# Relative-bias mask laid out on the host, stacks made in separate high and low steps, and the index scores of branch A moved by one projection unit

## The chip, the cores and the metric

The kernel runs on one core of a Trainium2 chip. The metric is the device time of one execution in microseconds (us), taken as the median of several runs; less is better. One execution of the kernel before was also recorded by the hardware profiler, and all rows below come from it.

## What is computed

Two layers of one block, on 512 positions of width 1024 in float32. A layer takes an RMS norm, projects it (`w_in`) and feeds three branches:

```
logits = einsum('bqhd,bsd->bqhs', iqb, ik)             # branch A, index scores: 4 heads of 64
score  = einsum('bqhs,bqh->bqs', relu(logits), iwb)    # the 128 best keys of each query are kept
s      = einsum(q, k_sel) * scale; softmax; times v    # branch A: 8 heads, 2 key heads
s      = einsum(q, k) * scale + bias[None]             # branch B: 8 heads, bias by relative position,
                                                       # keys of later 64-position chunks excluded
branch C: an mLSTM in chunks, 4 heads of 128
x + merge(branches, gates) @ w_out
```

## The kernel before, in words

**Units.** The projections of a layer are cut into units of 128 output columns (U_IQ = 0, U_IK = 2, U_SMALL = 3, U_AK = 4, U_AV = 5, U_AQ = 6 to 9, U_BQ = 10, U_BK = 14, U_BV = 18, the C branch from 22, the z gates of branch A from 34). A unit is 24 matmuls of 128x512 on TensorE (L565): the weights and the activations are each kept as a rounded high part and a low part that is the rest, and each of eight chunks takes high by high, low by high and high by low. ScalarE (ACT) makes the high part of a unit's weights (L756) two units ahead and reads a unit's sum out of PSUM (L819), in this order; GpSimd (POOL) makes the low part (L515).

**One hand-written order.** `schedule()` (L72 to L210) writes one list of steps for a layer, SEQUENCE, and every engine goes through this same list and does its own part of each step. `interleave()` (L213) puts the steps that stand between two units into the 24 matmuls of the later one, in groups separated by CUT, at even distances. So a step's place in the list sets its place in the queue of each engine at once. An attention item n (0 to 31 branch A, 32 to 63 branch B, head h = (n - 32) // 4 and query tile t = n % 4) is pushed by `push(n)` (L78): ("scores", n), then exp of item n - 1, the turning of n - 2 and the values of n - 3. TensorE's score banks in PSUM are two, used in turn: the scores of item n wait until VectorE (DVE) has read item n - 2.

**Stacks.** A score matmul contracts over 128 rows: 64 rows of high part and 64 rows of low part, stacked in `iq_s`, `ik_s`, `ak_s`, `aq_s`, `bq_s`, `bk_s`. In one step, such as ("b_stack", h), ACT writes the high parts (L879, L881, counted by `stack_hi`), and DVE waits for them and writes the low parts (L1131 to L1138, counted by `stack_ready`); TensorE waits for the latter (L618, L629, L635). The step stands at item 29 + 4h, and head h of branch B begins at item 32 + 4h. The index stacks (L847 to L858, L1105 to L1114) stand after units 5 and 6, and the index scores of query tile 1 inside unit 7 (L111, L115 to L121). The index scores of tiles 2 and 3 are inside units 13 and 15 (INDEX_AT). The first stacks of branch A stand after unit 16 (L136), the others at items 2, 10 and 18 (STACK_AT, L68).

**Top keys.** 48 rounds ("topk", L1139 to L1149) of the 8 largest scores and their replacement run on DVE: ROUNDS (L65) says how many stand behind each unit from 7 to 16, and the rest are spread over the items 0 to 21.

**Ropes.** ("rope", u) turns a projection by position with four DVE instructions of 128x512 and a shuffle (L1085 to L1088). That of U_AK stands right ahead of the first index scores, those of units 6 to 9 two units behind their unit.

**Bias.** ("rel_bias", h): ACT issues the DMA of a head's 128x512 bias (L898), for head 0 and 1 after unit 16, for a later head h at item 27 + 4h, where DVE must have read the last item of head h - 2. DVE, in the same step, waits for the DMA and writes the excluded corner of 64x64 with a memset (L1169, L1170). The scores step of branch B adds the bias and takes the row maximum (L1185).

Of the kernel before, what the change touches and what calls it, by code (L numbers as in the profile page):

```python
# [64 lines left out]
ROUNDS = {7: 4, 8: 4, 9: 4, 10: 4, 11: 0, 12: 2, 13: 2, 14: 2, 15: 2, 16: 2}  # L65


STACK_AT = {2: ("aq_stack", 1), 10: ("aq_stack", 2), 18: ("aq_stack", 3), 26: ("b_stack", 0)}  # L68
STACK_AT.update({29 + 4 * h: ("b_stack", h) for h in range(1, HEADS)})


def schedule():  # L72
# [184 lines left out]
STACK, STACKS = order("iq_stack", "ik_stack", "ak_stack", "aq_stack", "b_stack")  # L257
DVE_STEPS = 267
# [21 lines left out]
def build(nc, x_in, w_full, w_mix, params_in, rel_in, gains_in, consts_in, out, x_kept):  # L280
    ctx = ExitStack()
    with ctx:
# [255 lines left out]
        def _(pe):  # L538
# [49 lines left out]
            for l in range(DEPTH):  # L588
                for kind, n in SEQUENCE:
# [25 lines left out]
                    elif kind == "index":  # L615
                        t, h = n
                        bank = scores_bank(l, step)
                        pe.wait_ge(stack_ready, l * STACKS + STACK[("ik_stack", 0)] + 1)  # L618
# [4 lines left out]
                    elif kind == "scores":  # L623
# [3 lines left out]
                        if branch == "a":  # L627

                            pe.wait_ge(stack_ready, l * STACKS + STACK[("aq_stack", t)] + 1)  # L629
# [4 lines left out]
                        elif branch == "b":  # L634
                            pe.wait_ge(stack_ready, l * STACKS + STACK[("b_stack", h)] + 1)  # L635
# [97 lines left out]
        def _(act):  # L733
# [24 lines left out]
            for l in range(DEPTH):  # L758
# [64 lines left out]
                for kind, n in SEQUENCE:  # L823
# [23 lines left out]
                    elif kind == "iq_stack":  # L847
# [8 lines left out]
                    elif kind == "ik_stack":  # L856
                        act.wait_ge(roped, l * ROPES + ROPE[("rope", U_IK)] + 1)
                        act.activation(ik_s[:, 0, :], ik[:, :], ACT.Copy).then_inc(stack_hi, 1)  # L858
                    elif kind == "ak_stack":
# [6 lines left out]
                    elif kind == "aq_stack":  # L866
# [7 lines left out]
                    elif kind == "b_stack":  # L874
# [4 lines left out]
                        act.activation(bq_s[n % 2][b:b + HD, :], bq[b:b + HD, n // 2, :], ACT.Copy)  # L879
# [108 lines left out]
        def _(dve):  # L988
# [46 lines left out]
            for l in range(DEPTH):  # L1035
# [9 lines left out]
                for kind, n in SEQUENCE:  # L1045
# [59 lines left out]
                    elif kind == "iq_stack":  # L1105
                        dve.wait_ge(stack_hi, l * STACKS + STACK[step] + 1)
# [5 lines left out]
                    elif kind == "ik_stack":  # L1112
                        dve.wait_ge(stack_hi, l * STACKS + STACK[step] + 1)
                        dve.tensor_tensor(ik_s[:, 1, :], ik[:, :], ik_s[:, 0, :].bitcast(F32), ALU.subtract).then_inc(stack_ready, 1)  # L1114
                    elif kind == "ak_stack":
                        dve.wait_ge(stack_hi, l * STACKS + STACK[step] + 1)
# [6 lines left out]
                    elif kind == "aq_stack":  # L1123
                        dve.wait_ge(stack_hi, l * STACKS + STACK[step] + 1)
# [5 lines left out]
                    elif kind == "b_stack":  # L1130
                        dve.wait_ge(stack_hi, l * STACKS + STACK[step] + 1)  # L1131
                        p, q = (0, HD) if n % 2 == 0 else (HD, 0)
                        dve.tensor_tensor(bq_s[n % 2][q:q + HD, :], bq[p:p + HD, n // 2, :], bq_s[n % 2][p:p + HD, :].bitcast(F32),
                                          ALU.subtract)
# [295 lines left out]
```

## Time and profile before

| | us |
|---|---|
| median of 3 runs (1436.21 to 1438.34) | 1437.28 |
| the profiled execution, its own time | 1437.05 |
| its span in the trace | 1435.2 |
| TensorE, matmuls busy | 1326.3 (92%) |
| DVE busy | 758.3 (53%) |
| ACT busy | 624.5 (44%) |
| POOL busy | 480.5 (33%) |
| mean granted clock of TensorE | 0.967 of full speed |

The span runs from the first to the last recorded instruction, so about 2 us of the profiled execution lie around it. The first layer fills the trace up to about 725 us and the second, of the same steps, the rest; the stretch that the change touches goes from about 54 to 386 us, and again from about 750 to 1081 us.

### The profile page before, as it was taken

What the parts mean: (1) busy time and instruction counts of PE and PEld (TensorE: products, weight loads), DVE (VectorE), ACT (ScalarE), POOL (GpSimd) and SP (SyncE); (2) the same over time, 40 slices, a digit from 0 to 9 for tenths busy, and PEclk for the clock granted to TensorE, in tenths of its full rate; (3) what the DMA queues carried; (4) which work ended last, traced back from release to release, by engine and by line L of the source; (5) the groups of instructions that cost most, each with busy time, mean ns of one, the idle gap of its engine ahead of it and who ended that gap; (6) DMA issues with size and microseconds to landing.
All of it is one profiled execution on the core that took longest, in us unless ns stands there. A gap on an engine that the chain in (4) does not pass through costs nothing.

```text
span 1435.2 us, 20030 instructions
## 1 busy us (share of the span) xinstructions
PE 1326.3 (92%) x6525; PEld 1106.4 (77%) x6525; DVE 758.3 (53%) x1460; ACT 624.5 (44%) x1119; POOL 480.5 (33%) x227
## 2 busy tenths in 40 slices
PE   5989898779999899999998989888899989999997
PEld 3768787668898688888876878777778868888886
DVE  5788787664445421211868877757453461212156
ACT  4434555656543332332343356564654343322332
POOL 2533221221113344444553432221111234444442
PEclk9999999999999999999999999999999999999999
DMA  6222211112132133323242222111111313323331
GB/s 234 75 73 91 74 57 45 52 59 67 43 105 69 57 95 92 99 94 110 76 174 76 74 95 68 45 52 54 51 62 51 110 51 102 95 88 102 93 105 58
DMA packets 37034, 117.42 MB, mean 82 GB/s; under 512 B 4064, under 2 KB 6496, under 8 KB 36448
## 3 DMA queue, kind: packets, MB, share of 16 engines
q1 hardware_dynamic: 34368, 111.37, 23.6%
q10 hardware_dynamic: 2592, 5.11, 1.1%
q8 instruction: 40, 0.66, 0.2%
q14 instruction: 34, 0.28, 0.1%
HBM read 110.18 MB, written 6.29 MB: 81 GB/s over the span
## 4 chain that ended last, share of the span: by engine, by line
PE 66%; DVE 19%; issue 6%; ACT 4%; DMA 2%; POOL 1%; DVEq 0%; ACTq 0%; SPq 0%; POOLq 0%
PE acc L565 54%; PE ps_o L674 3%; PE ps_t L661 2%; DVE score L1146 2%; DVE top L1144 1%; PE ps_t L652 1%; DVE prob L1185 1%; PE ps_o L681 1%; DMA rel<-rel 1%; PE ps_s L631 1%; DVE bk_lo_s L1136 1%; DVE aq_s L1127 1%; DVE att_c L1286 1%; ACT bk_hi_s L881 1%; DVE turn L1160 1%
## 5 line engine op out<-in xcount | busy, mean ns | idle before, releaser
L515 POOL TENSOR_TENSOR w_lo<-w_raw,w_hi 128x1024 fp32r<-128x1024 f32 (+1 forms) x212 | 468.3, 2210 | 922.4 <-ACT w_hi L756 922.4
L565 PE MATMUL acc<-h_hi,w_hi 128*128 128x512 f32 x1136 | 465.4, 410 | 0.1
L565 PE MATMUL acc<-h_lo,w_hi 128*128 128x512 f32 x1136 | 456.0, 401 | 0.0
L565 PE MATMUL acc<-h_hi,w_lo 128*128 128x512 f32 x1136 | 302.6, 401 | 1.2 <-POOL w_lo L515 1.2
L756 ACT ACTIVATE w_hi<-w_raw 128x1024 fp32r<-128x1024 f32 (+1 forms) x212 | 203.9, 962 | 129.7 <-PE acc L565 99.5
L565 PEld LDWEIGHTS acc<-h_hi,w_hi 128*128 128x128 f32 x1136 | 220.0, 194 | 42.3 <-ACT w_hi L756 1.1
L565 PEld LDWEIGHTS acc<-h_lo,w_hi 128*128 128x128 f32 x1136 | 220.1, 194 | 41.1
L565 PEld LDWEIGHTS acc<-h_hi,w_lo 128*128 128x128 f32 x1136 | 212.7, 192 | 43.9 <-POOL w_lo L515 2.0
L1299 DVE SCALAR_TENSOR_TENSOR gated<-prob,acc 128x512 f32<-128x512 f32 x16 | 11.0, 688 | 251.8 <-PE acc L565 251.8
L904 ACT ACTIVATE prob<-prob,neg_max 128x128 f32<-128x128 f32 (+3 forms) x128 | 70.9, 554 | 71.2 <-DVE neg_max L1185 70.7
L954 ACT ACTIVATE prob<-acc,par_half 128x512 f32<-128x512 f32 x48 | 33.0, 688 | 154.1 <-PE acc L565 154.1
L661 PE MATMUL ps_t<-consts,prob 128*128 128x128 f32 x320 | 59.2, 284 | 18.8 <-ACT prob L904 18.7
L928 ACT ACTIVATE prob_t<-ps_t 128x128 f32<-128x128 f32 (+3 forms) x128 | 54.2, 423 | 45.1 <-PE ps_t L661 44.6
L674 PE MATMUL ps_o<-bv,prob_t 128*128 128x64 f32 x320 | 45.8, 276 | 21.6 <-issue 21.3
L1144 DVE MAX8 top<-score 128x8 f32<-128x256 f32 (+2 forms) x96 | 53.8, 561 | 17.5 <-DVE neg_max L1185 8.6
L674 PEld LDWEIGHTS ps_o<-bv,prob_t 128*128 128x128 f32 x320 | 43.3, 201 | 24.5 <-issue 23.0
L661 PEld LDWEIGHTS ps_t<-consts,prob 128*128 128x128 f32 x320 | 39.8, 145 | 28.5 <-issue 24.0
L674 PE MATMUL ps_o<-av,prob_t 128*128 128x64 f32 x320 | 44.9, 273 | 9.6 <-issue 9.6
L1146 DVE MATCH_REPLACE8 score<-top,score 128x256 f32<-128x256 f32 (+2 forms) x96 | 52.1, 543 | 0.0
L674 PEld LDWEIGHTS ps_o<-av,prob_t 128*128 128x128 f32 x320 | 42.5, 199 | 10.9 <-issue 10.8
L565 PE MATMUL acc<-merged_hi,w_hi 128*128 128x512 f32 x128 | 50.4, 394 | 0.3
L565 PE MATMUL acc<-merged_lo,w_hi 128*128 128x512 f32 x128 | 50.6, 395 | 0.0
(240 smaller groups left out, 1847.5 us busy)
## 6 DMA issues: line engine op xcount, KB each, us to landing
w_raw<-w_full SPq DMA_DIRECT2D x164, 512.0 KB, 3.4
w_raw<-w_mix SPq DMA_DIRECT2D x48, 256.0 KB, 2.6
x_kept<-xT SPq DMA_DIRECT2D x2, 2048.0 KB, 9.3
rel<-rel ACTq DMA_DIRECT2D x16, 256.0 KB, 2.7
xT<-x_kept SPq DMA_DIRECT2D x2, 2048.0 KB, 9.8
stage<-x SPq DMA_DIRECT2D x4, 512.0 KB, 6.9
out<-stage SPq DMA_DIRECT2D x4, 512.0 KB, 2.9
consts<-consts ACTq DMA_DIRECT2D x1, 640.0 KB, 4.1
```

What stands on the lines that cost most here:

```text
L515: pool.tensor_tensor(w_lo[:, slot, 0:nk, :], w_raw[:, raw, 0:nk, :], w_hi[:, slot, 0:nk, :].bitcast(F32), ALU.subtract).then_inc(split_ful ...
L565: last = pe.matmul(acc[slot][:, :], w[:, slot, k, :], x[:, k, :], start=(i == 0), stop=(i == 3 * nk - 1))
L631: last = pe.matmul(bank[:, 0:w], aq_s[:, t % 2, h, :], ak_s[:, h // BR, part, 0:w], start=(part == 0), stop=(part == 1))
L652: last = pe.matmul(ps_t[n % 2][:, s * P:(s + 1) * P], ck[:, h, s * P:(s + 1) * P], cq[:, h, t * P:w], start=True, stop=True)
L661: last = pe.transpose(ps_t[n % 2][:, s * P:(s + 1) * P], prob[:, n % 3, s * P:(s + 1) * P], ident)
L674: last = pe.matmul(ps_o[:, place * HD:(place + 1) * HD], prob_t[:, n % 2, s * P:(s + 1) * P], v[:, s, f:f + HD], start=(s == 0), stop=(s = ...
L756: act.activation(w_hi[:, slot, 0:nk, :], w_raw[:, raw, 0:nk, :], ACT.Copy).then_inc(w_hi_done, 1)
L904: act.activation(prob[:, n % 3, 0:(t + 1) * P], prob[:, n % 3, 0:(t + 1) * P], ACT.Exp, bias=neg_max[:, n % 4:n % 4 + 1], scale=-1.0, accu ...
L928: act.activation(prob_t[:, n % 2, 0:(t + 1) * P], ps_t[n % 2][:, 0:(t + 1) * P], ACT.Copy)\
L954: act.activation(prob[:, b, :], acc[b % 2][:, :], ACT.Tanh, bias=par_half[:, bass.ds(i * 2 + (C_GATE + DC * b + j), 1)], scale=0.5).then_i ...
L1144: link(dve.max(top8[:, :], s))
L1146: link(dve.match_replace(s, top8[:, :], s, TAKEN))
```

## The change

1. The host writes the excluded corner of the bias into the array that the DMA reads, and the rel_bias part of DVE goes. Its wait for the DMA moves to the scores of the head's first item (t = 0). ACT issues the DMAs where it did.
2. Each stack step is cut into a high step (ACT) and a low step (DVE) that stand at different places. For head h of branch B: bq_hi at item 28 + 4h, bk_hi and bq_lo at 29 + 4h, bk_lo at 30 + 4h (all were at 29 + 4h); for head 0: items 25, 26, 27 and 28 (was 26). For branch A's query tiles 1, 2 and 3: the high step at 2, 9, 17 and the low step at 4, 11, 19 (were 2, 10, 18). TensorE waits for the low step that comes last.
3. The index scores of tile 1 move from inside unit 7 to inside unit 8, the top-key rounds from units 7 to 16 to units 8 to 16 (four at unit 11 in place of none, none at 7), and every rope of units 6 to 9 by one unit; that of U_AK goes behind unit 8, thus behind the index scores. The small weights' turn (turn_iw) now comes before the index stacks' low steps in DVE's order. The first stacks of branch A are made ahead: high after unit 15, low after unit 16 and ahead of that unit's two rounds.

```diff
-ROUNDS = {7: 4, 8: 4, 9: 4, 10: 4, 11: 0, 12: 2, 13: 2, 14: 2, 15: 2, 16: 2}
-STACK_AT = {2: ("aq_stack", 1), 10: ("aq_stack", 2), 18: ("aq_stack", 3), 26: ("b_stack", 0)}
-STACK_AT.update({29 + 4 * h: ("b_stack", h) for h in range(1, HEADS)})
+ROUNDS = {8: 4, 9: 4, 10: 4, 11: 4, 12: 2, 13: 2, 14: 2, 15: 2, 16: 2}
+STACK_AT = {}
+for n, step in ((2, ("aq_hi", 1)), (4, ("aq_lo", 1)), (9, ("aq_hi", 2)), (11, ("aq_lo", 2)), (17, ("aq_hi", 3)), (19, ("aq_lo", 3)),
+                (25, ("bq_hi", 0)), (26, ("bk_hi", 0)), (27, ("bq_lo", 0)), (28, ("bk_lo", 0))):
+    STACK_AT[n] = [step]
+for h in range(1, HEADS):
+    for n, kind in ((28, "bq_hi"), (29, "bk_hi"), (29, "bq_lo"), (30, "bk_lo")):
+        STACK_AT.setdefault(n + 4 * h, []).append((kind, h))
...
     units(4, 6)
-    seq.append(("iq_stack", 0))
+    seq.append(("iq_hi", 0))
     units(6, 7)
-    seq.extend((("iq_stack", 1), ("ik_stack", 0)))
     seq.append(("turn_iw", 0))
-    seq.append(("rope", U_AK))
+    seq.extend((("iq_hi", 1), ("ik_hi", 0), ("iq_lo", 0), ("iq_lo", 1), ("ik_lo", 0)))
+    units(7, 8)
+    seq.append(("turn_v", U_AV))
     index(1)
...
-    for u in range(7, 17):
+    for u in range(8, 17):
         units(u, u + 1)
-        if u == U_AV + 2:
-            seq.append(("turn_v", U_AV))
-        if U_AQ <= u - 2 < U_BQ:
-            seq.append(("rope", u - 2))
+        if u == 8:
+            seq.append(("rope", U_AK))
+        if U_AQ <= u - 3 < U_BQ:
+            seq.append(("rope", u - 3))
         if u in INDEX_AT:
             index(INDEX_AT[u])
+        if u == 15:
+            seq.extend((("ak_hi", 0), ("aq_hi", 0)))
+        if u == 16:
+            seq.extend((("ak_lo", 0), ("aq_lo", 0)))
...
-    seq.extend((("ak_stack", 0), ("aq_stack", 0)))
...
-                    elif kind == "b_stack":
+                    elif kind == "bq_hi":
                         act.wait_ge(evac, evacs(l, U_BV - 1))
                         done = 23 if n == 0 else 27 + 4 * n
                         act.wait_ge(score_full, l * SCORE_USES + SCORE_USE[("scores", done)] + 1)
                         b = n % 2 * HD
-                        act.activation(bq_s[n % 2][b:b + HD, :], bq[b:b + HD, n // 2, :], ACT.Copy)
+                        act.activation(bq_s[n % 2][b:b + HD, :], bq[b:b + HD, n // 2, :], ACT.Copy).then_inc(stack_hi, 1)
+                    elif kind == "bk_hi":
...
-                    elif kind == "rel_bias":
-                        dve.wait_ge(rel_in_s[n % 2], l * 64 + 16 * (n // 2 + 1))
-                        link(dve.memset(rel[0:P // 2, n % 2, SEQ - P // 2:SEQ], NEG))
...
                             if branch == "b":
+                                if t == 0:
+                                    dve.wait_ge(rel_in_s[h % 2], l * 64 + 16 * (h // 2 + 1))
                                 mask = rel[:, h % 2, SEQ - w:SEQ]
...
     rel = a["rel_bias"][:, :, dist].reshape(-1, P, SEQ)
+    rel[:, 0:P // 2, SEQ - P // 2:SEQ] = NEG
```

The instructions of every stack are the ones of before; only their steps, their counters and their places differ.

## Rows read from the trace of the kernel before

**Rows 1.** Windows of the first layer: length, busy us and (x count) by engine, clock

```profile
150.25:220.49 70.24, 64.82 (x354) 54.96 (x355) 54.82 (x139) 37.69 (x93) 16.73 (x7) 0.96 0.19 61
220.49:264.83 44.34, 44.34 (x247) 38.29 (x247) 29.41 (x53) 24.92 (x49) 7.19 (x3) 0.93 0.11 37
264.83:326.65 61.82, 45.39 (x232) 38.09 (x232) 39.05 (x73) 32.96 (x71) 12.69 (x5) 0.89 0.19 60
326.65:386.00 59.35, 55.12 (x331) 47.40 (x331) 26.73 (x69) 36.85 (x80) 11.84 (x5) 0.97 0.17 54
```

**Rows 2.** Timeline of TensorE at its stops: start, us, instruction, [idle, releaser]

```profile
79.27 0.77 PE L620 MATMUL ps_s<-ik_s,iq_s 128*128 128x256 f32 x2 [5.54 <-DVE ik_s L1114]
...
80.27 0.63 PE L565 MATMUL acc<-h_lo,w_hi 128*128 128x512 f32 x1
80.69 0.63 PE L565 MATMUL acc<-h_hi,w_hi 128*128 128x512 f32 x1
...
150.25 0.66 PE L631 MATMUL ps_s<-ak_s,aq_s 128*128 128x128 f32 x2 [4.57 <-DVE aq_s L1127]
...
220.49 1.52 PE L674 MATMUL ps_o<-av,prob_t 128*128 128x64 f32 x6 [4.05 <-issue]
...
269.94 0.66 PE L661 MATMUL ps_t<-consts,prob 128*128 128x128 f32 x2 [5.11 <-ACT prob L904]
...
287.63 0.41 PE L674 MATMUL ps_o<-bv,prob_t 128*128 128x64 f32 x2 [3.61 <-issue]
...
305.70 0.41 PE L674 MATMUL ps_o<-bv,prob_t 128*128 128x64 f32 x2 [1.88 <-issue]
...
306.46 0.39 PE L565 MATMUL acc<-h_hi,w_hi 128*128 128x512 f32 x1
306.69 0.39 PE L565 MATMUL acc<-h_lo,w_hi 128*128 128x512 f32 x1
...
322.99 0.66 PE L674 MATMUL ps_o<-bv,prob_t 128*128 128x64 f32 x2 [4.46 <-issue]
```

**Rows 3.** Who waited for whom, both layers: total us, times, longest

```profile
DVE rel L1170 <- DMA rel<-rel: 36.0, 10, 6.4
...
DVE bq_s L1133 <- ACT bk_hi_s L881: 23.4, 13, 2.6
```

**Rows 4.** Timeline of DVE from the first index stacks to the second index scores

```profile
74.10 4.30 DVE L1109 TENSOR_TENSOR iq_s<-iq,iq_s 64x384 fp32r<-64x384 f32 x4
...
100.19 2.30 DVE L1086 TENSOR_TENSOR turn<-turn,consts 128x512 f32<-128x512 f32 x1
...
122.78 0.42 DVE L1097 TENSOR_SCALAR score<-prob,iw 128x384 f32<-128x384 f32 x1
...
125.51 0.56 DVE L1144 MAX8 top<-score 128x8 f32<-128x384 f32 x1 [0.16 <-DVE score L1104]
...
127.00 0.56 DVE L1144 MAX8 top<-score 128x8 f32<-128x384 f32 x1 [0.15 <-DVE score L1146]
```

**Rows 5.** Timeline of POOL beside one rope, then of ACT and TensorE at unit 15

```profile
99.56 2.39 POOL L515 TENSOR_TENSOR w_lo<-w_raw,w_hi 128x1024 fp32r<-128x1024 f32 x1 [2.91 <-ACT w_hi L756]
...
123.30 0.49 ACT L892 ACTIVATE prob<-ps_s 128x384 f32<-128x384 f32 x1 [6.74 <-DVE score L1097]
...
126.31 0.50 PE L565 MATMUL acc<-h_hi,w_hi 128*128 128x512 f32 x1
```

**Rows 6.** Timeline of DVE at the first stacks of branch A

```profile
143.85 2.79 DVE L1120 TENSOR_TENSOR ak_s<-ak,ak_s 64x512 fp32r<-64x512 f32 x4 [0.64 <-ACT ak_s L864]
146.67 3.43 DVE L1127 TENSOR_TENSOR aq_s<-aq,aq_s 64x512 fp32r<-64x512 f32 x2
```

**Rows 7.** Timeline of DVE and ACT around items 33 to 35

```profile
260.68 0.69 DVE L1133 TENSOR_TENSOR bq_s<-bq,bq_s 64x512 fp32r<-64x512 f32 x1 [2.50 <-ACT bk_hi_s L881]
261.29 1.39 DVE L1136 TENSOR_TENSOR bk_lo_s<-bk,bk_hi_s 64x512 fp32r<-64x512 f32 x2
...
269.20 0.51 ACT L904 ACTIVATE prob<-prob,neg_max 128x256 f32<-128x256 f32 x1
```

More of the change, by code:

```diff
@@ L149, in schedule @@
                 seq.append(work.pop(0))
-            if n in STACK_AT:
-                seq.append(STACK_AT[n])
+            seq.extend(STACK_AT.get(n, []))
             if n == 31:
@@ L256 @@
 ROPE, ROPES = order("rope")
-STACK, STACKS = order("iq_stack", "ik_stack", "ak_stack", "aq_stack", "b_stack")
-DVE_STEPS = 267
+STACK_HI, STACKS = order("iq_hi", "ik_hi", "ak_hi", "aq_hi", "bq_hi", "bk_hi")
+STACK_LO, _ = order("iq_lo", "ik_lo", "ak_lo", "aq_lo", "bq_lo", "bk_lo")
+DVE_STEPS = 259
 def item(n):
@@ L617, in _ @@
                         bank = scores_bank(l, step)
-                        pe.wait_ge(stack_ready, l * STACKS + STACK[("ik_stack", 0)] + 1)
+                        pe.wait_ge(stack_ready, l * STACKS + STACK_LO[("ik_lo", 0)] + 1)
                         for part in range(2):
@@ L627, in _ @@
                         if branch == "a":
-                            pe.wait_ge(stack_ready, l * STACKS + STACK[("aq_stack", t)] + 1)
+                            pe.wait_ge(stack_ready, l * STACKS + STACK_LO[("aq_lo", t)] + 1)
                             for part in range(2):
@@ L634, in _ @@
                         elif branch == "b":
-                            pe.wait_ge(stack_ready, l * STACKS + STACK[("b_stack", h)] + 1)
+                            pe.wait_ge(stack_ready, l * STACKS + STACK_LO[("bk_lo", h)] + 1)
                             for part in range(2):
@@ L846, in _ @@
                         act.activation(dst, spare[:, :].rearrange("p (t c) -> p t c", t=NT), ACT.Copy).then_inc(spare_free, 1)
-                    elif kind == "iq_stack":
+                    elif kind == "iq_hi":
                         if n == 0:
@@ L855, in _ @@
                         last.then_inc(stack_hi, 1)
-                    elif kind == "ik_stack":
+                    elif kind == "ik_hi":
                         act.wait_ge(roped, l * ROPES + ROPE[("rope", U_IK)] + 1)
                         act.activation(ik_s[:, 0, :], ik[:, :], ACT.Copy).then_inc(stack_hi, 1)
-                    elif kind == "ak_stack":
+                    elif kind == "ak_hi":
                         act.wait_ge(roped, l * ROPES + ROPE[("rope", U_AK)] + 1)
@@ L865, in _ @@
                         last.then_inc(stack_hi, 1)
-                    elif kind == "aq_stack":
+                    elif kind == "aq_hi":
                         act.wait_ge(roped, l * ROPES + ROPES)
@@ L878, in _ @@
                         b = n % 2 * HD
-                        act.activation(bq_s[n % 2][b:b + HD, :], bq[b:b + HD, n // 2, :], ACT.Copy)
+                        act.activation(bq_s[n % 2][b:b + HD, :], bq[b:b + HD, n // 2, :], ACT.Copy).then_inc(stack_hi, 1)
+                    elif kind == "bk_hi":
+                        b = n % 2 * HD
                         for p in (0, HD):
@@ L1104, in _ @@
                             link(dve.memset(score[0:P // 2, t % 2, w - P // 2:w], INADMISSIBLE))
-                    elif kind == "iq_stack":
-                        dve.wait_ge(stack_hi, l * STACKS + STACK[step] + 1)
+                    elif kind == "iq_lo":
+                        dve.wait_ge(stack_hi, l * STACKS + STACK_HI[("iq_hi", n)] + 1)
                         for p, q in ((0, HD), (HD, 0)):
@@ L1111, in _ @@
                         last.then_inc(stack_ready, 1)
-                    elif kind == "ik_stack":
-                        dve.wait_ge(stack_hi, l * STACKS + STACK[step] + 1)
+                    elif kind == "ik_lo":
+                        dve.wait_ge(stack_hi, l * STACKS + STACK_HI[("ik_hi", n)] + 1)
                         dve.tensor_tensor(ik_s[:, 1, :], ik[:, :], ik_s[:, 0, :].bitcast(F32), ALU.subtract).then_inc(stack_ready, 1)
-                    elif kind == "ak_stack":
-                        dve.wait_ge(stack_hi, l * STACKS + STACK[step] + 1)
+                    elif kind == "ak_lo":
+                        dve.wait_ge(stack_hi, l * STACKS + STACK_HI[("ak_hi", n)] + 1)
                         for kv in range(2):
@@ L1122, in _ @@
                         last.then_inc(stack_ready, 1)
-                    elif kind == "aq_stack":
-                        dve.wait_ge(stack_hi, l * STACKS + STACK[step] + 1)
+                    elif kind == "aq_lo":
+                        dve.wait_ge(stack_hi, l * STACKS + STACK_HI[("aq_hi", n)] + 1)
                         for p, q in ((0, HD), (HD, 0)):
@@ L1129, in _ @@
                         last.then_inc(stack_ready, 1)
-                    elif kind == "b_stack":
-                        dve.wait_ge(stack_hi, l * STACKS + STACK[step] + 1)
+                    elif kind == "bq_lo":
+                        dve.wait_ge(stack_hi, l * STACKS + STACK_HI[("bq_hi", n)] + 1)
                         p, q = (0, HD) if n % 2 == 0 else (HD, 0)
                         dve.tensor_tensor(bq_s[n % 2][q:q + HD, :], bq[p:p + HD, n // 2, :], bq_s[n % 2][p:p + HD, :].bitcast(F32),
-                                          ALU.subtract)
+                                          ALU.subtract).then_inc(stack_ready, 1)
+                    elif kind == "bk_lo":
+                        dve.wait_ge(stack_hi, l * STACKS + STACK_HI[("bk_hi", n)] + 1)
+                        p = n % 2 * HD
                         for o in (0, HD):
```

## The prediction

> **What bounds the kernel now.** I read the windows first [rows 1], then TensorE's own stops [rows 2], then who waited for whom [rows 3], and last the queues of DVE and ACT ahead of each stop [rows 4 to 7]. TensorE is the bound: outside the stretch from 54 to 386 us, and its twin in the second layer, this change moves nothing, so only TensorE's idle time and its half clock inside that stretch can be won. Between 264.83 and 326.65 it is busy for 45.39 of 61.82 us; between 220.49 and 264.83 for all of it; between 326.65 and 386.00 it idles for 4.2 us [rows 1]. The stops to see in rows 2 are 5.54 (index scores, on DVE's low part), 4.57 (first scores of branch A, again on a low part), 4.05, 5.11, 3.61, 1.88 and 4.46 us. A long stop has a second price: behind the one at 79.27 the matmuls of 512 columns start 0.42 us apart (80.27 to 80.69 [rows 2]), which is 1.2 GHz, while behind the stop of 1.88 us at 305.70 they start 0.23 apart (306.46 to 306.69 [rows 2]), which is 2.4 GHz (24 matmuls, a unit, then take 5.44 us). The ten or so at half clock lose 0.2 each, about 2.0 us. The half clock follows stops of 3.61 us and more, and not that of 1.88.
>
> Behind the stops stands DVE. Between 264.83 and 326.65 it is busy for 39.05 of 61.82 us, and much of the rest it waits with work queued behind it: 36.0 us in both layers for the bias DMA and 23.4 us for ACT's high parts of branch B [rows 3].
>
> **Part 1, index scores one unit later.** Removed is the stop of 5.54 and 2.0 of half clock. TensorE reaches the index scores after 24 more matmuls, 5.44 us later, so at about 79.2; DVE's low parts, 4.30 for the four of iq_s [rows 4] and ik_s behind them, are done by about 79.1, as now, since TensorE went on at 79.27 [rows 2] (turn_iw's copy goes ahead of them, but the first one waited for POOL anyway). So TensorE leaves unit 8 about 7.3 us ahead. This does not last. From the index scores to 122.78 DVE has hardly a gap: ropes and 16 rounds. In the new order it idles between the four index scores, which TensorE hands over one per 1.15 us, and the rope of U_AK, which used to fill such time, comes after them. I put DVE's end of index plus rope 0.8 us later than now, and against it the collisions told below, so the second index scores come no earlier than now, at 122.0 give or take 1.5. ACT waits there for DVE in order (6.74 us [rows 5]), and behind it are queued the reading of unit 13 and the weights of unit 15. TensorE starts unit 15 3.53 us after DVE's L1097 (122.78 and 126.31 [rows 4, 5]), so at 125.5 after the change, a gain of 0.8. It now arrives at 119.2: a new stop of about 6.3 us, with 2.0 of half clock behind it. **The first stop is moved, not removed.**
>
> The give or take is a collision. The rope's L1086 at 100.19 took 2.30 us [rows 4] because POOL's split ran from 99.56 for 2.39 [rows 5]; at other places it takes 0.69. With five ropes and a split per unit I leave the number of collisions as it is. The Trainium skill, "SBUF — State Buffer", has the rule: a DVE operation with two SBUF inputs and a GpSimd operation that reads SBUF exclude each other for the whole instruction, and the one that comes second waits. By that rule retimed ropes can collide in other places, none to five; the trace agrees.
>
> **Part 2, first stacks of branch A made ahead.** Two rounds of 1.47 us (125.51 to 127.00 [rows 4]) go behind them and the wait of 0.64 for ACT [rows 6] goes: DVE ends aq_lo at 150.1 - 2.9 - 0.6 - 0.8 = 145.8. ACT's high parts, 3.8 us, fit between units 15 and 16, where it idles. TensorE comes at 145.7 (its arrival now) - 0.8 + 2.0 = 146.9: no stop. It issues at 146.9 in place of 150.25 [rows 2], 3.3 us earlier, and saves 2.0 of half clock behind. But from here to 220.49 DVE is the slower (54.82 busy of 70.24, and its own 0.2 us links between most instructions [rows 1]); it is ahead by 3.3 to 4.5. The stop of 4.05 at 220.49 stays. I take **4.0 us** at 220.49 and keep it to 264.83, where TensorE is never idle. Bounds: 0.5 (collisions eat it) and 6.
>
> **Part 3, branch B's stacks in two steps, no wait for the bias.** At item 33 DVE no longer waits 2.50 for bk_hi [rows 7], so its first row step reaches ACT some 3.2 us earlier, and with it the exp at 269.20 that ended the stop of 5.11 [rows 2, 7]: about 1.9 stays, short enough for full clock. The longest wait for the bias, 6.4 for head 2 [rows 3], falls between items 35 and 36 and goes: at item 40 the DMA has long landed. What of the waits between items 33 and 48 goes is 2.5 + 6.4 and another five of 0.8 to 2.9, 20 us in all. DVE's walk over these items, from its scores at 257.8 to those at 326.9, is then 69 - 20 = 49 us. TensorE's is 69 less its stops of 16 (idle 16.4 in rows 1) and half clock behind three of them, 4.8, so 48. The two are equal, so TensorE can follow closely; DVE may not be more than two items late. Of the 20.8 I take off 1.9 for the exp that stays and 2 for items at which both are late: **17 us**. Bounds: 8 (only the two stops at 269.94 and 287.63 shrink, each with its half clock) and 21. Who is late next: bk_lo, one item later than before. Its 1.39 us [rows 7] now stand behind the scores of item 30 + 4h and ahead of TensorE's 32 + 4h; while TensorE is less than two items ahead this is hidden.
>
> **Part 4, 326.65 to 386.** Here TensorE idles for 4.2 [rows 1] while DVE waits for the bias and bk_hi as well. I take **2 us**, bounds 0 and 4. The sixteen memsets of 0.11 are in the waits. The DMAs are issued where they were, and SP's and POOL's queues get nothing new.
>
> **Sum.** 4 + 17 + 2 = 23 us a layer by these steps; I take 2 off for row steps and stacks that meet POOL's splits in a stretch where neither engine has slack, so 21. Both layers show the same waits (twice the first layer's [rows 3]), so 42. Against the profiled execution's own 1437.05 this gives 1395; the median of 1437.28 differs by 0.2, and I say **1396**.
>
> **Rivals.** (a) Branch B gives less. TensorE's stops there are then made by ACT's order (exp behind table load, weights and sums) and not by DVE's waits; the exp at 269.20 speaks for it, DVE's lateness against. Part 3 gives its lower bound 8, part 2 its 2: 10 a layer, **1417**. (b) The first stop is really gone, since DVE has room before unit 15: then part 1 gives 7.3 that reaches 220.49, as far as DVE's rounds let it, some 5 more a layer, with part 3 at its upper bound: 30 a layer, **1377**. The 6.74 that ACT waits at 123.30 speaks against. (c) Slower. bk_lo is the last arrival: TensorE runs two items ahead, stands at item 32 + 4h until DVE has done scores 30 + 4h (0.8) and bk_lo (1.4). Alone this is 2.2 us for each of seven heads; it decides against the change only if each such stop joins another and brings half clock as well, 2.2 + 1.6 = 3.8, so 27 a layer against a gain of 21: 12 us slower, **1449**. Against it: DVE loses 20 us of waits in the same place. (d) The waits that go are hidden anyway and each is replaced by the next one; parts 1 and 2 come to nothing: **1436**. TensorE's idle 16.4 us in that window [rows 1] speaks against.
>
> **Chances.** The forecast 0.58, (a) 0.21, (b) 0.12, (c) 0.04, (d) 0.05. The forecast's own parts move it by 9 us or so a side (part 2's and part 3's bounds, both layers). With most of (a) and (b) inside, the range is 1376 to 1419. A measurement of this kernel tells a change from none at about 0.2%, 3 us. Faster: the forecast, (a) and (b), 0.91. Same: (d), 0.05. Slower: (c), 0.04.
>
> **What would show it.** TensorE's stop ahead of L620 is under 1 us and a stop of 5 to 7 us stands ahead of unit 15, released by ACT's weights, with matmuls at half clock behind. L631's first stop is gone. DVE shows no wait for a DMA of the bias and next to none at bq_lo. Between the scores of item 33 and item 48 lie about 52 us in place of 69. The exp of item 33 still stands behind a table load. Wrong would be: the second index scores on DVE several us earlier than 122 (b), stops of TensorE at L637 released by bk_lo (c), or the same span between items 33 and 48 with ACT as releaser (a, d).

## The result and the profile after

The changed kernel takes 1399.93 us (median of 4 runs, 1398.23 to 1404.01), against 1437.47 for the kernel before (4 runs, 1436.21 to 1438.34): a ratio of 0.9744, 95% interval 0.9721 to 0.9766, or 37.5 us less. The forecast was 1396 in 1376 to 1419. The profiled execution of the changed kernel is the slowest of its four, 1404.01, with a span of 1402.2 us. The busy times of the engines on its page:

```profile
PE 1314.3 (94%) x6525; PEld 1094.7 (78%) x6525; DVE 768.9 (55%) x1444; ACT 623.5 (44%) x1119; POOL 482.2 (34%) x227
```

TensorE issues the same 6525 matmuls in 12 us less of busy time (less half clock), and idles for 87.9 us of the span in place of 108.9. DVE has 16 instructions fewer, the memsets, and is yet busy 10.6 us longer.

Windows of the first layer, columns as in [rows 1]. The first ends at the new stop; the other four answer to the four there:

```profile
54.00:128.00 74.00, 65.58 (x297) 54.05 (x296) 61.07 (x117) 25.26 (x36) 27.92 (x12) 0.96 0.26 86
152.50:219.00 66.50, 60.02 (x341) 51.36 (x341) 52.29 (x136) 37.71 (x93) 17.55 (x8) 0.99 0.20 64
219.00:263.00 44.00, 44.00 (x247) 37.95 (x247) 30.79 (x57) 27.56 (x53) 7.19 (x3) 0.93 0.11 37
263.00:310.00 47.00, 41.01 (x226) 34.23 (x226) 38.77 (x64) 28.46 (x64) 12.35 (x5) 0.96 0.20 62
310.00:370.00 60.00, 58.03 (x360) 50.08 (x358) 31.33 (x72) 40.35 (x87) 12.28 (x6) 1.00 0.20 67
```

Most of the time came out of the window from 263 to 310: 6.0 us of TensorE idle at a clock of 0.96, in place of 16.4 at 0.89. In the stretch before it, from 219, TensorE is never idle, as before. DVE is now busy 38.77 of 47.00 us in the same place: what went are its waits, not its work.

TensorE at its stops [rows 2]:

```profile
80.27 0.40 PE L629 MATMUL ps_s<-ik_s,iq_s 128*128 128x256 f32 x2
...
127.62 0.80 PE L574 MATMUL acc<-h_hi,w_hi 128*128 128x512 f32 x1 [8.41 <-ACT w_hi L765]
...
149.21 0.36 PE L640 MATMUL ps_s<-ak_s,aq_s 128*128 128x128 f32 x2
...
218.88 1.51 PE L683 MATMUL ps_o<-av,prob_t 128*128 128x64 f32 x6 [3.22 <-issue]
...
265.02 0.41 PE L670 MATMUL ps_t<-consts,prob 128*128 128x128 f32 x2 [2.01 <-ACT prob L915]
...
266.04 0.63 PE L574 MATMUL acc<-h_hi,w_hi 128*128 128x512 f32 x1
266.47 0.63 PE L574 MATMUL acc<-h_lo,w_hi 128*128 128x512 f32 x1
...
288.48 0.44 PE L646 MATMUL ps_s<-bk_hi_s,bq_s 128*128 128x384 f32 x1 [0.61 <-DVEq L1202]
...
297.42 0.30 PE L646 MATMUL ps_s<-bk_hi_s,bq_s 128*128 128x128 f32 x1 [1.69 <-DVE bk_lo_s L1150]
```

The stops of 5.54 and 4.57 us are gone (80.27 and 149.21 have none), a new one of 8.41 stands ahead of unit 15, and in place of 5.11, 3.61, 1.88 and 4.46 stand 2.01, 0.61, 1.69 and nothing over 1 us up to 370. Another new stop, of 2.31 us, stands at 167.91. In the second layer of this execution one more is left that the first has not:

```profile
956.84 0.41 PE L683 MATMUL ps_o<-bv,prob_t 128*128 128x64 f32 x2 [2.72 <-issue]
```

Who waited for whom, both layers [rows 3]:

```profile
ACT prob L903 <- DVE score L1108: 29.0, 2, 14.5
...
DVE bq_s L1144 <- PE ps_o L683: 5.3, 8, 1.1
...
PE ps_s L646 <- DVE bk_lo_s L1150: 4.4, 3, 1.7
```

No wait of DVE for a DMA of the bias is left, and for ACT at the stacks of branch B only two of 0.2 us each. Four rows of DVE and two of POOL, ahead of the first index scores and behind them:

```profile
79.25 0.69 DVE L1125 TENSOR_TENSOR ik_s<-ik,ik_s 128x512 fp32r<-128x512 f32 x1
81.12 1.62 DVE L1108 TENSOR_SCALAR score<-prob,iw 128x256 f32<-128x256 f32 x1 [1.17 <-ACT prob L903]
...
87.79 2.77 DVE L1099 TENSOR_TENSOR ak<-ak,turn 128x512 f32<-128x512 f32 x1
...
104.34 2.06 DVE L1097 TENSOR_TENSOR turn<-turn,consts 128x512 f32<-128x512 f32 x1
```

```profile
80.18 2.41 POOL L524 TENSOR_TENSOR w_lo<-w_raw,w_hi 128x1024 fp32r<-128x1024 f32 x1 [3.09 <-ACT w_hi L765]
87.12 2.89 POOL L524 TENSOR_TENSOR w_lo<-w_raw,w_hi 128x1024 fp32r<-128x1024 f32 x1 [4.53 <-ACT w_hi L765]
```

The rope of U_AK met a split of POOL, and so did the first instruction on the index scores (1.62 for what takes 0.35 in the kernel before, at 82.46). A later rope, at 104.34, met the split at 103.46 (2.06 for 0.69). The kernel before has two such collisions in the same stretch, the one at 100.19 [rows 4] and this one:

```profile
110.49 2.88 DVE L1087 TENSOR_TENSOR aq<-aq,consts 128x512 f32<-128x512 f32 x1
```

Then DVE at the second index scores, at the first stacks of branch A, and its score steps of items 33 and 48:

```profile
124.11 0.42 DVE L1108 TENSOR_SCALAR score<-prob,iw 128x384 f32<-128x384 f32 x1
...
145.54 3.47 DVE L1138 TENSOR_TENSOR aq_s<-aq,aq_s 64x512 fp32r<-64x512 f32 x2
...
256.21 0.42 DVE L1198 CUSTOM_DVE_ANT_0 prob<-ps_s,rel 128x256 f32<-128x256 f32 x1 [0.23 <-PE ps_t L670]
...
311.53 0.29 DVE L1198 CUSTOM_DVE_ANT_0 prob<-ps_s,rel 128x128 f32<-128x128 f32 x1 [0.45 <-PE ps_t L670]
```

### The profile page after: what moved, and what is told of

Same layout as the page of the kernel before. It is cut to its first block, busy times and chain, and to the rows that moved or that the text cites. A ratio compares the mean times of both kernels' runs of the same rounds, so it can differ in the third digit from the quotient of the medians.

```text
span 1402.2 us, 20000 instructions
## 1 busy us (share of the span) xinstructions
PE 1314.3 (94%) x6525; PEld 1094.7 (78%) x6525; DVE 768.9 (55%) x1444; ACT 623.5 (44%) x1119; POOL 482.2 (34%) x227
## 3 DMA queue, kind: packets, MB, share of 16 engines
q10 hardware_dynamic: 2592, 5.11, 1.2%
## 4 chain that ended last, share of the span: by engine, by line
PE 69%; DVE 20%; issue 5%; ACT 3%; POOL 1%; DVEq 0%; DMA 0%; ACTq 0%; SPq 0%; POOLq 0%
PE acc L574 56%; PE ps_o L683 3%; DVE score L1160 3%; DVE top L1158 2%; PE ps_t L670 2%; PE ps_t L661 1%; PE ps_o L690 1%; DVE prob L1198 1%; DVE bk_lo_s L1150 1%; PE ps_s L640 1%; DVE turn L1174 1%; DVE att_c L1299 1%; PE spare L700 1%; DVE turn L1097 1%; DVE aq_s L1138 1%
## 5 line engine op out<-in xcount | busy, mean ns | idle before, releaser
L574 PE MATMUL acc<-h_hi,w_hi 128*128 128x512 f32 x1136 | 459.3, 404 | 16.8 <-ACT w_hi L765 16.8
L574 PE MATMUL acc<-h_lo,w_hi 128*128 128x512 f32 x1136 | 450.1, 396 | 0.0
L574 PEld LDWEIGHTS acc<-h_hi,w_hi 128*128 128x128 f32 x1136 | 216.6, 191 | 58.9 <-ACT w_hi L765 18.1
L574 PEld LDWEIGHTS acc<-h_lo,w_hi 128*128 128x128 f32 x1136 | 216.4, 191 | 40.5
L915 ACT ACTIVATE prob<-prob,neg_max 128x128 f32<-128x128 f32 (+3 forms) x128 | 70.9, 554 | 56.1 <-DVE neg_max L1198 55.8
L670 PEld LDWEIGHTS ps_t<-consts,prob 128*128 128x128 f32 x320 | 39.5, 142 | 19.7 <-issue 15.0
L1198 DVE CUSTOM_DVE_ANT_0 prob<-ps_s,rel 128x128 f32<-128x128 f32 (+1 forms) x64 | 31.4, 490 | 36.5 <-PE ps_s L646 17.2
L1312 DVE SCALAR_TENSOR_TENSOR z<-prob,acc 128x512 f32<-128x512 f32 x32 | 22.0, 687 | 50.7 <-PE acc L574 50.7
```

Source lines behind the costliest of these rows:

```text
L574: last = pe.matmul(acc[slot][:, :], w[:, slot, k, :], x[:, k, :], start=(i == 0), stop=(i == 3 * nk - 1))
L670: last = pe.transpose(ps_t[n % 2][:, s * P:(s + 1) * P], prob[:, n % 3, s * P:(s + 1) * P], ident)
L915: act.activation(prob[:, n % 3, 0:(t + 1) * P], prob[:, n % 3, 0:(t + 1) * P], ACT.Exp, bias=neg_max[:, n % 4:n % 4 + 1], scale=-1.0, accu ...
L1198: dve.tensor_tensor_reduce(out=prob[:, n % 3, 0:w], in0=ps_s[use % 2][:, 0:w], in1=mask, scale=-1.0, scalar=3.0e38, op0=ALU.add, op1=ALU.m ...
L1312: dve.scalar_tensor_tensor((gated, z, z)[b][:, :], prob[:, b, :], 1.0, acc[(3 + b) % 2][:, :], ALU.add, ALU.mult)\
```

## The experiments

There are twelve kernels, every one measured against runs of the kernel before on the same chip (medians 1437.1 to 1437.8). The table gives each median, and for the profiled execution the time from DVE's score step of one item to that of another in layer 1 (differences of start times on its timeline).

| kernel | us | ratio, 95% interval | 0 to 24 | 33 to 48 | 48 to 63 |
|---|---|---|---|---|---|
| before | 1437.3 | | 74.6 | 69.2 | 53.2 |
| counters_only | 1428.4 | 0.9913 to 0.9946 | 74.6 | 68.1 | 50.1 |
| mask_only | 1413.7 | 0.9822 to 0.9862 | 74.8 | 62.3 | 49.7 |
| split_only | 1407.9 | 0.9777 to 0.9809 | 75.7 | 64.5 | 45.9 |
| order_only | 1426.1 | 0.9903 to 0.9936 | 73.3 | 67.7 | 49.9 |
| no_mask | 1408.8 | 0.9774 to 0.9808 | 72.0 | 64.5 | 45.9 |
| no_split | 1412.9 | 0.9804 to 0.9841 | 73.4 | 60.4 | 49.6 |
| no_order | 1402.0 | 0.9736 to 0.9776 | 75.6 | 55.3 | 48.9 |
| after | 1399.9 | 0.9721 to 0.9766 | 72.0 | 55.3 | 48.9 |
| bk_early | 1409.9 | 0.9794 to 0.9827 | 72.0 | 55.9 | 53.4 |
| rounds_late | 1401.7 | 0.9742 to 0.9778 | 71.3 | 55.4 | 48.9 |
| rounds_cut | 1380.6 | 0.9589 to 0.9624 | 72.2 | 55.3 | 48.9 |
| rows_first | 1412.0 | 0.9805 to 0.9837 | 73.7 | 56.5 | 49.1 |
| rows_bk_early | 1419.3 | 0.9858 to 0.9892 | 73.7 | 53.2 | 54.7 |

A profiled execution is one of four and need not be a typical one. That of the changed kernel lies 4.1 us above its median; in its second layer items 33 to 48 take 56.1 us and items 48 to 63 take 50.8, where no_order and rounds_late have 55.2 and 48.8. Those of counters_only and split_only lie 4.7 and 5.8 us above theirs.

**One part alone.** Each of the first three makes one edit of the diff in the kernel before; all three also count the high and the low steps apart, as the diff does.

mask_only, the host's corner and the wait at the first item:

```diff
-                    elif kind == "rel_bias":
-                        dve.wait_ge(rel_in_s[n % 2], l * 64 + 16 * (n // 2 + 1))
-                        link(dve.memset(rel[0:P // 2, n % 2, SEQ - P // 2:SEQ], NEG))
+                                if t == 0:
+                                    dve.wait_ge(rel_in_s[h % 2], l * 64 + 16 * (h // 2 + 1))
```

> The kernel before with part 1 of the change alone: corner of the bias written by the host, DVE's wait for the bias DMA moved to the head's first scores. My theory (DVE's waits in branch B are what stops TensorE): the 36 us of DVE waits go, those for ACT's bk_hi (23 us) stay; TensorE's stops between items 36 and 48 shrink by some 8 to 10 us a layer, the stop of 5.1 at item 33 stays. 1417 to 1421. Rival (each wait that goes is replaced by the next one, for bk_hi): above 1430. Rival (the mask is nearly everything): below 1410.

Measured 1413.68: 23.6 us less, 3.3 below the range of the theory and in neither rival's. TensorE's stop at item 33 is 4.45 (5.11 before).

split_only, the new STACK_AT with the mask and the order of before:

```diff
-STACK_AT.update({29 + 4 * h: ("b_stack", h) for h in range(1, HEADS)})
+    for n, kind in ((28, "bq_hi"), (29, "bk_hi"), (29, "bq_lo"), (30, "bk_lo")):
+        STACK_AT.setdefault(n + 4 * h, []).append((kind, h))
```

> The kernel before with the stacks of branch B, and the second to fourth of branch A, in separate high and low steps, nothing else. My theory: bk_hi waits go (23 us on DVE), the exp of item 33 comes some 3 us earlier, but DVE still stands at each bias DMA, issued by ACT: 4 to 6 us a layer, 1426 to 1430. Rival (waits replace each other): DVE waits longer for the bias by as much, 1434 to 1438.

Measured 1407.94, 29.4 us less: a miss by 18. The same edit moves the later stacks of branch A, and no run separates the two; items 0 to 24 take 75.7 and 72.4 us in the two layers with it, 74.6 and 74.3 without (counters_only). DVE still waits 32.6 us for the bias, and that costs TensorE little:

```profile
267.99 0.41 PE L666 MATMUL ps_t<-consts,prob 128*128 128x128 f32 x2 [2.01 <-ACT prob L911]
...
284.81 0.41 PE L679 MATMUL ps_o<-bv,prob_t 128*128 128x64 f32 x2 [2.74 <-issue]
```

These are TensorE's stops at item 33 and behind it, in place of 5.11 and 3.61 [rows 2]. The stop at item 33 tells the kernels apart: 4.40 to 4.45 us in the five that have bk_lo ahead of the first row step on DVE (counters_only, mask_only, order_only, no_split, bk_early) and 2.01 in those that have it behind (split_only, no_mask, no_order, after), with or without the mask. bk_early, told below, is the changed kernel but for the place of the bk steps:

```profile
266.55 0.66 PE L670 MATMUL ps_t<-consts,prob 128*128 128x128 f32 x2 [4.40 <-ACT prob L915]
```

order_only, part 3 of the diff in the kernel before:

> The kernel before with part 3 alone: index scores, ropes and rounds one unit later, first stacks of branch A ahead. The first stop (5.54) goes and one of 7 to 9 us stands ahead of unit 15; the stop of 4.57 goes. My theory: 2 to 4 us a layer are won, 1429 to 1433. Rival (the first stop is really gone): 1420 or less. Rival (nothing, DVE's work up to item 23 sets the time): 1436 to 1438.

Measured 1426.08, 11.2 us less, 2.9 below the range of the theory. The three gains sum to 64 us where the whole change has 37.5. Before that can be called overlap, what the three share must be taken out.

**The counters alone.** Every step at its old place, and only this, in branch B (each stack of branch A was counted by itself already):

```diff
-                        act.activation(bq_s[n % 2][b:b + HD, :], bq[b:b + HD, n // 2, :], ACT.Copy)
+                        act.activation(bq_s[n % 2][b:b + HD, :], bq[b:b + HD, n // 2, :], ACT.Copy).then_inc(stack_hi, 1)
...
-                        dve.wait_ge(stack_hi, l * STACKS + STACK[step] + 1)
+                        dve.wait_ge(stack_hi, l * STACKS + STACK_HI[("bq_hi", n)] + 1)
...
+                        dve.wait_ge(stack_hi, l * STACKS + STACK_HI[("bk_hi", n)] + 1)
```

> The kernel of before with only the semaphore's steps counted apart for the first and the second of each pair of stacks, every step at its old place. ScalarE may then end the second stack's copy while VectorE makes the first one's rest. Theory 'the places do it': 1434 to 1438, no difference. Rival 'the finer counting does a part of it': the four steps of a stack of branch B are released two and two, which takes the wait for bq_s (5 to 7 us a layer in the rows of before and of the mask alone) down: 1425 to 1432.

Measured 1428.39: the rival is right, and the finer counting is worth 9 us with nothing moved. Its waits of DVE, both layers:

```profile
DVE rel L1177 <- DMA rel<-rel: 40.3, 12, 6.4
...
DVE bq_s L1137 <- ACT bq_s L881: 9.7, 8, 1.5
DVE bk_lo_s L1143 <- ACT bk_hi_s L885: 2.7, 6, 0.5
```

The 23.4 us for ACT [rows 3] became 12.4. Before, DVE waited for three copies of ACT and then made both low parts; now it makes bq_s's while ACT copies the high parts of bk. Its interval leaves 8 to 12 us for the gain. The profiled execution is only 3.9 us shorter (spans 1431.3 and 1435.2), but items 33 to 63 gain 4.1 us in the first layer and 5.9 in the second; the rest was lost again outside the stretch that the edit touches. Counted from this kernel the places of the split give 20.5 us alone, the mask 14.7, the order 2.3.

**One part taken out.** no_order is the changed kernel with the list, the ropes and the rounds of before:

> The changed kernel without part 3: parts 1 and 2 alone, index scores and first stacks where they were. DVE's waits of branch B are all gone here. If the parts simply add on different stretches, this stands some 5 to 11 us above the changed kernel (order_only won 11.2): 1405 to 1411. Rival: the order's gain is lost once DVE has no waits left, 1399 to 1402.

Measured 1402.01, 2.1 us above the changed kernel, nearer to what the rival said. The stops of 5.54 and 4.56 are back, and items 0 to 24 take 3.6 us more in layer 1, but in the profiled executions layer 2 gives none of it (72.5 us without the order, 73.7 with it).

no_split has the high and the low steps of each stack at one place:

> The changed kernel with the high and low steps of branch B and of the later stacks of branch A back at one place, counters still separate. DVE waits for ACT's high parts again (about 8 us a layer). If the waits for the bias and for bk_hi replace each other, this is close to the changed kernel plus little, 1401 to 1406. If the split alone is what wins, it goes back to near mask_only, 1408 to 1413.

Measured 1412.88: the split is worth 13.0 on top of the rest. TensorE's stop at item 33 goes back to 4.44.

no_mask writes the corner on DVE again:

> The changed kernel without the mask's layout: VectorE waits for each bias tile and writes its corner itself again; the split and the order stay. Single parts gave -23.6 (mask alone), -29.4 (split alone) and -11.2 us (order alone), 64 together where the whole change gives 37.5, so they overlap. Theory 'each wait of VectorE counts': the waits for the bias come back in full (14.7 us a layer stood in the split's own run) and lengthen branch B, so 1418 to 1428. Theory 'the split lets TensorE run through these waits': the time goes back only by what layer 1 shows between split alone and the whole change at item 48 (270.4 against 257.8, of which the order gives some), a part of which is made up by item 63: 1405 to 1412, about 1407, near split alone (1408) or a few us below it.

Measured 1408.83, 8.9 us above, as the second theory said. DVE waits 31.6 us for the bias once more.

So against the kernel with the finer counters (1428.4) the mask gives 14.7 or 8.9, the split 20.5 or 13.0 and the order 2.3 or 2.1, alone or last. Alone they sum to 37.5, and together they give 28.5: mask and split win some 9 us of the same time. no_order, which has just these two, shows it directly: 26.4 us where 14.7 and 20.5 make 35.2.

**DVE's floor ahead of the scores.** rounds_late takes the rounds from unit 11 to units 12 and 13:

```diff
-ROUNDS = {8: 4, 9: 4, 10: 4, 11: 4, 12: 2, 13: 2, 14: 2, 15: 2, 16: 2}
+ROUNDS = {8: 4, 9: 4, 10: 4, 11: 0, 12: 4, 13: 4, 14: 2, 15: 2, 16: 2}
```

> The changed kernel with the four rounds behind unit 11 moved behind units 12 and 13, thus behind the second index scores. If DVE's lateness at the second index scores makes the stop ahead of unit 15, it falls from 8.4 to about 3.6. Where that time goes tells the floor: if DVE's total work up to item 23 is the bound (my theory), the stop appears again ahead of item 0 and the time changes by under 3 us in all (1397 to 1402); if the stop was the only loss, 4 to 6 us a layer are won, 1388 to 1392.

Measured 1401.71, no difference clear of noise. The stop changes its place; TensorE, two stops of this kernel:

```profile
121.11 0.79 PE L574 MATMUL acc<-h_hi,w_hi 128*128 128x512 f32 x1 [3.28 <-ACT w_hi L765]
...
149.45 0.66 PE L640 MATMUL ps_s<-ak_s,aq_s 128*128 128x128 f32 x2 [6.75 <-DVE aq_s L1138]
```

By itself this does not settle the floor. DVE's low parts ahead of item 0 met two splits here instead of one (8.33 us for the two stacks where the changed kernel has 6.26, told at the end), so up to 2.1 us a layer may have been lost that way. A clearer measure is DVE's own time from the low part of ik_s to the score step of item 0 in layer 1: 72.7 us before, 72.8 in the changed kernel, 72.6 in no_order, 74.5 here.

rounds_cut is the changed kernel without the last 8 of the 16 rounds of query tile 1; this leaves out part of the computation, since branch A then takes too many keys for that tile.

> The changed kernel with the last 8 of the 16 top-key rounds of query tile 1 left out, so branch A of that tile takes too many keys. It takes 9.7 us of DVE's work a layer out ahead of unit 15 and changes no other engine. If DVE's total work up to item 23 is the floor, the stop of 8.4 us ahead of unit 15 goes with the half clock behind it, nothing comes in its place, and 8 to 11 us a layer are won: 1378 to 1384. If TensorE or ACT bounds that stretch, at most 3 us a layer: 1394 or more.

Measured 1380.63 (ratio 0.9589 to 0.9624), 19.3 us less, 9.65 a layer. Eight rounds at 1.21 us (MAX8 at 118.37 and 119.58 on DVE's timeline) are 9.7. The stop ahead of unit 15 is 0.86, and one of 1.47 stands ahead of item 0. DVE's time from ik_s to item 0 is 64.5 us, 8.3 less, although its stacks and ropes lose 2.1 us more to splits than in the changed kernel. So from the first index scores to item 0 DVE's queue is the bound: work taken off it comes back nearly in full, and work moved within it (no_order, and rounds_late as far as it goes) hardly at all.

**Is bk_lo the one that is late?** bk_early has bk_hi at 28 + 4h and bk_lo at 29 + 4h:

> The changed kernel with bk_hi at item 28 + 4h and bk_lo at 29 + 4h, one item earlier each. The stop of 1.7 us ahead of the first scores of a head, released by bk_lo (item 40), should go. My theory: DVE's order only shifts, 0 to 2 us a layer: 1396 to 1400. Rival (bk_lo is a bound of its own): 5 us a layer or more, below 1391.

Measured 1409.87, 10 us slower: a miss. The stops for bk_lo went, and others grew: that of item 33 from 2.01 to 4.40, and most of the loss is in items 48 to 63 (53.4 us in place of 48.9). The largest stop there is 3.25 us. DVE, then ACT, then TensorE ahead of it:

```profile
346.54 1.39 DVE L1150 TENSOR_TENSOR bk_lo_s<-bk,bk_hi_s 64x512 fp32r<-64x512 f32 x2
347.96 0.69 DVE L1240 SCALAR_TENSOR_TENSOR z<-z_tanh,z 128x512 f32<-128x512 f32 x1
348.69 0.69 DVE L1244 SCALAR_TENSOR_TENSOR gated<-z,spare 128x512 f32<-128x512 f32 x1
...
349.47 0.69 ACT L788 ACTIVATE z_tanh<-acc,par_half 128x512 f32<-128x512 f32 x1 [6.22 <-DVE gated L1244]
...
350.98 1.06 ACT L765 ACTIVATE w_hi<-w_raw 128x1024 fp32r<-128x1024 f32 x1 [0.24 <-ACT z L789]
351.94 0.49 ACT L915 ACTIVATE prob<-prob,neg_max 128x256 f32<-128x256 f32 x1
...
352.67 0.41 PE L670 MATMUL ps_t<-consts,prob 128*128 128x128 f32 x2 [3.25 <-ACT prob L915]
```

The same place in the changed kernel:

```profile
344.76 0.69 DVE L1244 SCALAR_TENSOR_TENSOR gated<-z,spare 128x512 f32<-128x512 f32 x1
...
345.54 0.69 ACT L788 ACTIVATE z_tanh<-acc,par_half 128x512 f32<-128x512 f32 x1 [2.86 <-DVE gated L1244]
...
347.25 1.39 DVE L1150 TENSOR_TENSOR bk_lo_s<-bk,bk_hi_s 64x512 fp32r<-64x512 f32 x2
...
348.01 0.49 ACT L915 ACTIVATE prob<-prob,neg_max 128x256 f32<-128x256 f32 x1
```

With bk_lo ahead of the gating of a unit, ACT waits longer to read the next unit, and behind that stand, in its queue, the weights' high part and the exp for which TensorE waits. In the changed kernel bk_lo stands behind the gating, and the exp keeps 0.70 of the stop. That is what the new place of bk_lo buys, for one wait of 1.69 at 297.42.

rows_first moves one step, ("rows", 0), whose Exp and Ln bring two table loads of 1.28 us ahead of the exp of item 33, from item 31 to right behind unit 3:

> The changed kernel with the first step of the row sums of branch B's bias (Exp and Ln on ScalarE, with their two table loads) moved from item 31 to behind unit 3, where ScalarE has room. Theory 'the stop ahead of item 33 (2.01 us in layer 1, about as much in layer 2) is ScalarE's late exp behind those steps': that stop goes, and the table loads no longer stand in branch B: 1392 to 1398. Rival 'the step only moves, and its loads now delay evictions among the units': 1399 to 1404.

Measured 1411.99 (0.9805 to 0.9837), 12 us slower, beyond both theories. The stop of 2.01 goes, and 0.82 and 2.73 come at 279 to 284 (items 33 to 48 take 56.5). In its new place the step makes DVE late for the index scores: ik_s's low part ends at 83.89 in place of 79.94. The step's own instruction is 1.55 us of DVE; and the instructions behind it, shifted by it, met three splits, two in the ropes (2.77 at 68.83 and 2.34 at 74.67 for 0.69) and one in ik_s's low part itself, 5.8 us in all, where the changed kernel loses 2.6 in that stretch (1.79 for 0.49 at 69.81, 3.59 for 2.27 at 75.64). DVE, then TensorE:

```profile
81.12 2.77 DVE L1126 TENSOR_TENSOR ik_s<-ik,ik_s 128x512 fp32r<-128x512 f32 x1
...
84.03 0.48 PE L630 MATMUL ps_s<-ik_s,iq_s 128*128 128x256 f32 x2 [3.67 <-DVE ik_s L1126]
```

This stop stands in both layers (3.67 and 3.68), 7.4 us in all. The profiled executions differ by 7.4 as well (spans 1409.6 and 1402.2), the medians by 12.1, since the changed kernel was profiled 4.1 us above its median and this one 0.5 below.

rows_bk_early makes both moves:

> Both moves: the stacks of bk one item earlier (which by itself cost 10 us: 1409.9 against 1399.9) and the first row step behind unit 3. Theory 'the earlier bk steps cost time because they delay the row step on VectorE, and with it ScalarE's Exp, Ln and the exp of item 33 (its stop grew from 2.01 to 4.40)': with the row step gone from there the loss goes to a third or less, 1392 to 1402. Rival 'they cost time wherever they stand ahead of the score steps of VectorE': 8 to 10 us above the run with the first row step moved alone.

Measured 1419.27 (0.9858 to 0.9892): 7.3 us above rows_first. Without the row step the turning of item 33 has no stop any more with the early bk_lo, where it had 4.40, so there the row step was what bk_lo delayed. (A stop of 2.05 at 271.56, ahead of the item's values, is another one: DVE's scores of item 34 came late behind an instruction that took 2.76 us beside a split, at 267.05, and 0.75 in rows_first.) But the stop behind the gating stands as it was, 3.25. In layer 1 the early bk steps cost 1.3 us between items 24 and 33 and 5.6 between 48 and 63, and win 3.3 between 33 and 48. The rival comes nearer: most of the loss is not the row step's. No kernel here that does the whole computation beats the changed one; rounds_late and no_order come out equal to it within their intervals.

## Why the prediction held, step by step

**Part 1: "the first stop is moved, not removed".** As written. TensorE came to unit 15 at 119.21 (127.62 - 8.41; forecast 119.2) and started 3.51 us after DVE's L1108 (124.11), where the step had 3.53. Only DVE's arrival was off: 124.11 for 122.0 give or take 1.5, so the stop was 8.4 and not 6.3. The step's own terms do not give 122.0: 0.8 later with the collisions left as they are is 123.6, and 122.0 needs 1.6 us of collisions to go. The 0.8 held (the rope of U_AK ends at 90.56, 4.16 us after the end of index work and rope in the kernel before, 86.40, and 3.35 of that are two collisions). The collisions did not go: they cost 3.8 us in two places before and 4.7 in three now (1.27 at 81.12, 2.08 at 87.79, 1.37 at 104.34), 0.9 more. So the collisions were the term that failed, in number and in size.

By the Trainium skill, "SBUF — State Buffer", section "Who interferes with whom", an operation in a two-port mode, which tensor_scalar can be, contends like one with two SBUF inputs; the trace agrees: the one at 81.12 ended at 82.74, just behind POOL's split (82.59). The prediction had used half of that rule.

**Part 2: "no stop" at the first scores, 4.0 us to 220.49.** There is no stop, but the scores came at 149.21, not 146.9, for the same 2.1 us that TensorE started unit 15 late. It was close: DVE's aq_lo ended at 149.01 (145.54 and 3.47), 3.2 us later than forecast, by the same 2.1 and by waits of 0.77 and 0.41 for ACT at the index scores of tile 3, which the step did not have. Items 0 to 24 gained 2.6 us in layer 1 for 4.0, next to nothing in layer 2 (73.7 for 73.9), and the two runs that price the order by itself give 2.3 and 2.1 us for both layers where the sum had 8; each is within its uncertainty of nothing. The term was mis-sized: the step credited TensorE's earlier issue, though it said that from there on DVE is the slower, and TensorE's lead ended in the new stop of 2.31 at 167.91. The stop of 4.05 stayed, as 3.22.

**Part 3: 17 us.** The exp of item 33 left 2.01 (forecast 1.9), but not for the reason given alone: bk_early has no wait for bk_hi either and keeps 4.40, so bk_lo's place behind the row step was needed too. 20 us of DVE's waits went, and 55.3 us lie between the scores of items 33 and 48 in place of 69.2: 13.9 gained for 17 (52 forecast). What was taken for slack was partly not: DVE is busy for 38.77 of 47.00 us, and TensorE still had stops of 0.6 to 1.7. "Short enough for full clock" failed too: behind the 2.01 the matmuls start 0.43 apart (266.04 to 266.47). bk_lo was next, as said, but only three times in both layers, 4.4 us in all; rival (c) had the place and not the price. Rival (a) had 8 us here, for 13.9.

**Part 4: 2 us.** From item 48 to 63 it was 4.3 (53.2 to 48.9). Counters_only, which moves nothing, has 3.0 of that. Finer counting as a gain of its own, 9 us in both layers, was in no step of the prediction.

**The sum.** Items 33 to 63 gave 18.2 us in layer 1 for 19, items 0 to 24 gave 2.6 for 4, and item 0 itself comes 1.0 later on DVE (152.07 for 151.10); item 63 then comes 19.7 earlier (360.39 for 380.10). By the medians the change gives 18.8 a layer for 21. That the number came so near is in part luck: parts 2 and 3 were too high by 1.4 and 3.1, part 4 too low by 2.3, and the deduction of 2 for collisions stood in the sum. What each edit gives was less well known: by the runs the split is the largest part (13.0 or 20.5), not the wait for the bias (8.9 or 14.7). Rival (a) was nearer than the forecast for part 2 (2 us), and the stop of item 33 does hang on ACT's order, as it said, but the rest of branch B did not. Rival (b) fell by the 14.5 us that ACT waits ahead of unit 15, (d) by the window from 263 to 310.

## What to carry to other kernels

When a producer makes several things under one counter, count them apart before anything is moved: it cost no instruction here and gave 9 us (8 to 12). In an in-order queue ask of each step what stands right behind it: a low part of 1.39 us, where it stood ahead of the gating that lets ACT read the next unit, went with a loss of 4.5 us in items 48 to 63 of a layer, and with next to none one item later, although its own reader then waited up to 1.69. Where an engine has no slack, moving its work moves the stop (rounds_late, no_order), and here only taking work off it shortens the time (rounds_cut).

## What the runs showed of the hardware

The length of a stop of TensorE does not by itself tell the clock behind it. Behind 2.01 (changed kernel, 265.02) and 2.12 (kernel before, 366.89) matmuls of 512 columns start 0.43 apart, which is 1.2 GHz; behind 2.31 (changed kernel, 167.91) and 2.05 (split_only, 296.72) they start 0.23 to 0.24 apart, which is 2.4 GHz. The same stop of 2.01 in the second layer of the same execution (941.93) is followed by 0.23. Nor is it a narrow range: behind 1.91 in rounds_cut (158.46) they start 0.43 apart, and behind the 3.67 of rows_first 0.23:

```profile
84.35 0.40 PE L575 MATMUL acc<-h_hi,w_hi 128*128 128x512 f32 x1
84.58 0.40 PE L575 MATMUL acc<-h_lo,w_hi 128*128 128x512 f32 x1
```

DVE's work can take far longer by where it meets POOL. In rounds_late the low part of ak_s, 2.79 us [rows 6], met two splits; DVE, then POOL:

```profile
140.95 6.94 DVE L1131 TENSOR_TENSOR ak_s<-ak,ak_s 64x512 fp32r<-64x512 f32 x4
...
141.52 5.12 POOL L524 TENSOR_TENSOR w_lo<-w_raw,w_hi 128x1024 fp32r<-128x1024 f32 x2 [3.30 <-ACT w_hi L765]
```

And DVE's busy time went from 758.3 to 768.9 us with the same instructions less sixteen memsets, while in bk_early, again the same instructions, it was 756.8. The traces show where it goes. In the changed kernel 54 instructions of DVE took over 0.3 us more than the shortest one of the same operation, tiles and shape, 94 us in all, and each of the 54 overlaps an instruction of POOL; in the kernel before it is 48 and 84 us, in bk_early 46 and 80 us, again all of them. No run here prevents these collisions, so what they cost the kernel's time is not shown.
